# Cross attention's matmuls in three fp32r products of halves, another order of the first loads, and the last FFN's sums in one product each

## What is computed

```
for layer in 0, 1:
    x += 0.5 * ffn(rms_norm(x, g1))          # w_gu 1024 x 5632, w_down 2816 x 1024
    x += mixer(rms_norm(x, g2))              # attention, even or odd form
    x += cross(rms_norm(x, g3), rms_norm(mem, g4))
    x += 0.5 * ffn(rms_norm(x, g5))
x = second_block(x)                          # index attention, rnn, then an FFN

def cross(h, m):                             # m: 256 rows; 4 heads of 256
    q = rms_norm(h @ w_q, q_gain);  k, v = split(m @ w_kv);  k = rms_norm(k, k_gain)
    p = softmax(q @ k.T / 16)                # 512 x 256 per head
    return (p @ v) @ w_o
```

## Time and profile before

| | us |
|---|---|
| median of 3 runs | 3139.92 (3139.75 to 3141.52) |
| profiled execution, its own time | 3140.26 |
| its span in the trace | 3138.5 |
| TensorE busy in the span | 3117.4 |
| VectorE busy | 1580.1 |
| ScalarE busy | 1219.5 |
| cross stage of layer 0, on TensorE | about 678.8 to 712.3 |
| cross stage of layer 1, on TensorE | about 1819.7 to 1853.2 |

### The profile page before, as it was taken

One profiled execution on the slowest core, in us unless ns is written; L12 is line 12 of the kernel. 1 busy time (PEld: TensorE's weight loads), 2 busy tenths in 40 slices (PEclk: granted clock), 3 DMA queues, 4 the chain that ended last, 5 costly groups with the idle time before them and its releaser, 6 DMA issues.

```text
span 3138.5 us, 37126 instructions
## 1 busy us (share of the span) xinstructions
PE 3117.4 (99%) x14528; PEld 2520.7 (80%) x14528; DVE 1580.1 (50%) x2478; ACT 1219.5 (39%) x2001; POOL 314.4 (10%) x452
## 2 busy tenths in 40 slices
PE   9999999999999999999999999999999999999999
PEld 8888886887888888888866878888887786788887
DVE  4443348754444344433465754443346876564433
ACT  4332347543332233223465543332335727433222
POOL 1000114211000000001210200000142200020000
PEclk9999999999999999999999999999999999999999
DMA  4332331422333233323222413332232230223332
GB/s 152 99 96 95 100 94 35 141 68 88 101 95 100 94 94 94 101 99 96 88 94 81 148 49 99 100 96 96 84 101 81 81 108 28 88 80 95 96 99 74
DMA packets 213664, 290.95 MB, mean 93 GB/s; under 512 B 12880, under 2 KB 137168, under 8 KB 213360
## 3 DMA queue, kind: packets, MB, share of 16 engines
q1 hardware_dynamic: 210992, 279.59, 28.4%
q0 software_dynamic: 2496, 8.98, 0.9%
HBM read 286.42 MB, written 2.10 MB: 92 GB/s over the span
## 4 chain that ended last, share of the span: by engine, by line
PE 93%; issue 3%; ACT 1%; POOL 1%; DVE 1%; DMA 0%; SPq 0%; POOLq 0%; DVEq 0%
PE ps L94 91%; PE ps L97 3%; POOL evQ L142 0%; ACT sxPb L100 0%; ACT ocPb L100 0%; POOL evPb L142 0%; DMA x_rows<-in_x 0%; ACT sxPa L100 0%; ACT ocPa L100 0%; POOL evPa L142 0%; DVE ocPa L106 0%; DVE sxPa L106 0%; DVE evQ L115 0%; ACT ocPT L100 0%; ACT sxPT L100 0%
## 5 line engine op out<-in xcount | busy, mean ns | idle before, releaser
L103 DVE TENSOR_TENSOR wl<-raw,wh 128x1024 fp32r<-128x1024 f32 (+1 forms) x530 | 653.8, 1241 | 1070.9 <-ACT wh L100 1068.3
L100 ACT ACTIVATE wh<-raw 128x1024 fp32r<-128x1024 f32 (+1 forms) x530 | 551.7, 1050 | 1146.2 <-PE ps L94 1108.6
L94 PE MATMUL ps<-hTh,wh 128*128 128x512 f32 x2400 | 943.2, 393 | 1.8 <-DVE hTl L109 1.8
L94 PE MATMUL ps<-hTh,wl 128*128 128x512 f32 x2400 | 937.4, 391 | 0.0
L94 PE MATMUL ps<-hTl,wh 128*128 128x512 f32 x2400 | 937.3, 391 | 0.0
L94 PEld LDWEIGHTS ps<-hTh,wh 128*128 128x128 f32 x2400 | 450.9, 188 | 104.7 <-issue 11.0
L94 PEld LDWEIGHTS ps<-hTh,wl 128*128 128x128 f32 x2400 | 450.8, 188 | 96.9 <-issue 5.0
L94 PEld LDWEIGHTS ps<-hTl,wh 128*128 128x128 f32 x2400 | 450.9, 188 | 96.0 <-issue 5.9
L103 POOL TENSOR_TENSOR xn<-xn 128x512 f32<-128x512 f32 x67 | 95.9, 1431 | 1768.4 <-ACT xn L100 1529.6
L94 PE MATMUL ps<-wh,hTh 128*128 128x512 f32 (+2 forms) x576 | 217.4, 377 | 0.9 <-DVE s_ikT L121 0.9
L94 PE MATMUL ps<-wh,hTl 128*128 128x512 f32 (+2 forms) x576 | 216.0, 375 | 0.0
(11 more groups left out here) (418 smaller groups left out, 4068.1 us busy)
## 6 DMA issues: line engine op xcount, KB each, us to landing
raw<-in_ffn_w_gu SPq DMA_DIRECT2D x352, 256.0 KB, 3.1
raw<-in_ffn_w_down SPq DMA_DIRECT2D x88, 512.0 KB, 3.5
raw<-in_xa_w_kv SPq DMA_DIRECT2D x32, 512.0 KB, 3.9
raw<-in_w_in SPq DMA_DIRECT2D x28, 512.0 KB, 3.7
raw<-in_od_w_in SPq DMA_DIRECT2D x24, 512.0 KB, 3.6
raw<-in_w_ffn_gate SPq DMA_DIRECT2D x44, 256.0 KB, 2.8
raw<-in_w_ffn_up SPq DMA_DIRECT2D x44, 256.0 KB, 3.1
raw<-in_w_ffn_down SPq DMA_DIRECT2D x22, 512.0 KB, 3.8
```

The source lines that it names most:

```text
L94: return self.made(lambda e: e.matmul(*a, **k))
L100: return self.made(lambda e: e.activation(*a, **k))
L103: return self.made(lambda e: e.tensor_tensor(*a, **k))
```

## The change

- *Cross attention.* `qT`, `kT`, `v` and `PT` become pairs of fp32r tiles, upper and lower. ScalarE writes all upper halves, VectorE all lower halves, each after ScalarE's (`act_halves`, `dve_halves`, `act_whole_turned`, `dve_whole_turned`). Each fp32 matmul of scores and values becomes three fp32r products. `P` and `PT` move to memory that is free by then.
- *Order of products.* In group 0 of every GEMM the two products with the activations' upper half come first for all columns, and wait for the upper half only; the one with the lower half comes after.
- *Start.* SP loads x's first quarter, half a chunk of weights and x's second quarter, then waits for x's first quarter; ScalarE's own queue loads the other half of chunk 0, the identity and the first gains. Chunk 0 is split in halves. Two chunks of x are turned before the first product, two after product 12, four after product 36; 14 matmuls on ones.
- *Last FFN.* GpSimd adds all eight squares, and TensorE makes 4 matmuls in place of 12, after product 82.

```diff
     def sp_weights(sp):
+        sp.dma_start(x_rows[:, :, 0:256], x_in_rows[:, :, 0:256]).then_inc(x_in[0], 0, 16)
+        first_weights(sp, 1)
+        sp.dma_start(x_rows[:, :, 256:512], x_in_rows[:, :, 256:512]).then_inc(x_in[1], 0, 16)
+        sp.wait_ge(x_in[0], 0)
...
+    def act_loads(act):
+        first_weights(act, 0)
+        act.dma_start(ident, T["misc"][:, 0:P]).then_inc(ident_in, 0, 16)
+        act.dma_start(prm[:, 0:8], T["prm"][:, 0:8]).then_inc(prm_in, "first gain", 16)
...
+                if not g and len(block) == 1:
+                    order = [(k, j, qs) for k in ks for qs in ([range(3)] if k[0] == K - 1 else [range(2), range(2, 3)])
+                             for j in range(len(jobs))]
...
-        pe_warm(pe, home["f1u0", 0], 18)
-        pe_turn_x(pe, range(4))
-        pe_gemm(pe, "f1u0", {"h": hT("f1u0")}, side)
+        pe_warm(pe, home["f1u0", 0], 14)
+        pe_turn_x(pe, range(2))
+        side = rates_side(pe_rates, pe, "f1u0")
+        for i, _ in enumerate(pe_products(pe, "f1u0", {"h": hT("f1u0")}, side), 1):
+            if i == 12:
+                pe_turn_x(pe, range(2, 4))
+            elif i == 36:
+                pe_turn_x(pe, range(4, KD))
...
+    def act_whole_turned(act, A, h):
+        for n in range(2):
+            act.wait_ge(turned, (A.tag, h, n))
+            if h >= 2:
+                act.wait_ge(valued, (A.tag, h - 2))
+            for d_, s_ in whole_blocks(A, h, n, 0):
+                ins = act.activation(d_, s_, AF.Copy)
+            ins.then_inc(put, (A.tag, h, n, "hi"))
+
+    def dve_whole_turned(dve, A, h):
+        for n in range(2):
+            dve.wait_ge(put, (A.tag, h, n, "hi"))
+            if h >= 2:
+                dve.wait_ge(valued, (A.tag, h - 2))
+            for (d_, s_), (hi, _) in zip(whole_blocks(A, h, n, 1), whole_blocks(A, h, n, 0)):
+                ins = dve.tensor_tensor(d_, s_, hi.bitcast(F32), ALU.subtract)
+            ins.then_inc(put, (A.tag, h, n)).also(drained, (A.tag, h, "t", n))
...
+    def act_halves(act, name, g, nt, dst, gain):
+        for c in range(4):
+            act.wait_ge(turned, (name, g, c))
+            act.activation(dst[0][:, 4 * (g % 2) + c, :], bank[home[name, g] + c][:, 0:nt * P], AF.Copy,
+                           scale=gain[:, c % 2:c % 2 + 1]).then_inc(put, (name, g, "hi", c))
+
+    def dve_halves(dve, name, g, nt, dst, gain):
+        for c in range(4):
+            dve.wait_ge(put, (name, g, "hi", c))
+            dve.scalar_tensor_tensor(dst[1][:, 4 * (g % 2) + c, :], bank[home[name, g] + c][:, 0:nt * P],
+                                     gain[:, c % 2:c % 2 + 1], dst[0][:, 4 * (g % 2) + c, :].bitcast(F32), ALU.mult,
+                                     ALU.subtract).then_inc(put, (name, g, "T", c)).also(drained, ("turn", name, g, c))
...
-                ins = pe.matmul(dst, C.qT[:, u, i * P:(i + 1) * P], C.kT[:, u, :], start=c == 0, stop=c == 1)
+                for n, (a, b) in enumerate(((0, 0), (0, 1), (1, 0))):
+                    ins = pe.matmul(dst, C.qT[a][:, u, i * P:(i + 1) * P], C.kT[b][:, u, :], start=c == 0 and n == 0,
+                                    stop=c == 1 and n == 2)
...
-        pe_gemm(pe, "f3u", {"h": hT("f3u")}, rates_side(pe_rates, pe, "f3u"))
+        side = rates_side(pe_rates, pe, "f3u")
+        for i, _ in enumerate(pe_products(pe, "f3u", {"h": hT("f3u")}, side), 1):
+            if i == 82:
+                pe_sums(pe, "f3u", rate_bank("f3u"), [(total, step, ("f3u", "sum", KD - 1))], (1,))
...
-        pool_sums(pool, "f3u", KD - 2)
+        pool_sums(pool, "f3u")
```

More of the change, by code:

```diff
@@ L400, in sp_weights, with act_first, dve_first @@
                 o += width
+    def act_first(act, kk):
+        key = 0 if kk else "half"
+        act.wait_ge(raw_in[0], key)
+        act.activation(wh[0][:, kk, 0:chunk(0)], raw[0][:, kk, 0:chunk(0)], AF.Copy).then_inc(w_hi, key)
+        act.split = 1
+    def dve_first(dve, kk):
+        key = 0 if kk else "half"
+        dve.wait_ge(raw_in[0], key)
+        dve.wait_ge(w_hi, key)
+        dve.tensor_tensor(wl[0][:, kk, 0:chunk(0)], raw[0][:, kk, 0:chunk(0)], wh[0][:, kk, 0:chunk(0)].bitcast(F32),
+                          ALU.subtract).then_inc(w_lo, key)
+        dve.split = 1
     def act_split(act, upto):
@@ L622, in pe_rates @@
     def pe_rates(pe, N, g, kp):
[L623 to L627, removed]
+        if (g, kp) == (0, 2) and N not in ("f1u0", "f3u"):
+            pe_sums(pe, N, rate_bank(N), [(total, step, (N, "sum", KD - 1))], (1,))
         if (g, kp) == (0, 3) and N not in no_spread:
@@ L680, in upper @@
             act.wait_ge(turned, ("x", c))
-            act.wait_ge(prm_in, 0)
+            act.wait_ge(prm_in, "first gain")
             act_hi(act, bank[x_bank(c)][:, :], hT("f1u0"), c, slice(0, S), None, norm_gain["f1u0"][:, c:c + 1])
         def square(t):
-            act.wait_ge(x_in[0], 0)
-            act.wait_ge(x_in[1], 0)
+            for part in x_in:
+                act.wait_ge(part, 0)
             if t:
@@ L713, in keep @@
             dve.tensor_copy(xT[:, c, :], bank[x_bank(c)][:, :]).then_inc(x_ready, ("x", c)).also(drained, ("x", c))
-        dve_split(dve, 0)
-        for c in (0, 1, 2, 3):
+        dve_first(dve, 0)
+        lower(0)
+        dve_first(dve, 1)
+        lower(1)
+        for c in (0, 1):
+            keep(c)
+        dve_split(dve, 1)
+        for c in (2, 3):
             lower(c)
-        keep(0)
-        dve_split(dve, 1)
-        for c in (1, 2, 3):
+        for c in (2, 3):
             keep(c)
@@ L1276, in pe_whole, with whole_blocks @@
                 value(pe, s - 2, A.pt[s % 2])
[L1278 to L1282, removed]
+    def whole_blocks(A, h, n, u):
+        src, at = bank[A.tv + n], 0
+        for i in A.groups[n]:
+            k0, k1, _, W = WHOLE[i]
+            yield A.pt[h % 2][u][:, k0:k1, i * P:(i + 1) * P], src[:, at:at + W].rearrange("p (k q) -> p k q", k=k1 - k0)
+            at += W
+    def act_whole_turned(act, A, h):
[14 more added lines that the diff above has]
+            ins.then_inc(put, (A.tag, h, n)).also(drained, (A.tag, h, "t", n))
     def act_whole(act, A, finish, then):
@@ L1946, in side @@
             if (g, kp) == (3, 1):
[L1947 removed]
+                act_halves(act, C.kv, 2, 2, C.kT, C.kgain)
         def evict(g):
@@ L1973, in evict @@
                 return
[L1974 to L1977 removed]
+            for t in range(2):
+                cols = slice(512 * g, 512 * (g + 1))
+                dve.wait_ge(put, (C.kv, "vh", g, t))
+                dve.tensor_tensor(C.vl[:, t, cols], bank[home[C.kv, g] + t][:, :], C.vh[:, t, cols].bitcast(F32),
+                                  ALU.subtract).then_inc(put, (C.kv, "v", g, t)).also(drained, (C.kv, g, t))
         dve_gemm(dve, C.kv, evict, side)
@@ L2054, in value @@
                 for kt in range(2):
-                    ins = pe.matmul(bank[b][:, :], C.v[:, kt, 256 * h + c * P:256 * h + (c + 1) * P], PTb[:, kt, :],
-                                    start=kt == 0, stop=kt == 1)
+                    cols = slice(256 * h + c * P, 256 * h + (c + 1) * P)
+                    for n, (v, p) in enumerate(((C.vh, 0), (C.vl, 0), (C.vh, 1))):
+                        ins = pe.matmul(bank[b][:, :], v[:, kt, cols], PTb[p][:, kt, :], start=kt == 0 and n == 0,
+                                        stop=kt == 1 and n == 2)
                 ins.then_inc(valued, (A.tag, h, c)).also(valued, (A.tag, h))
```

116 lines of the change are left out of this document (59 added, 57 removed).

## The result

The changed kernel takes 3148.64 us (median of 13 runs, 3146.95 to 3151.27), the kernel before beside it 3141.31 us (3138.70 to 3144.88). The ratio is 1.0023, with an interval of 1.0015 to 1.0030: slower by about 7 us, where 8.3 were forecast. The profiled execution has a span of 3145.2 us, 6.7 more than before.

The account below looks back on a forecast made before the run. TensorE was busy 3117.4 of 3138.5 us, but the ScalarE-VectorE loop was taken to decide the cross stage. Cross stages +14.2, start -3.5, last FFN -2.4 gave +8.3 on 3140.26: 3148.5, as median 3148.2 us; range 3143.5 to 3154.5.

Parts of the forecast that it names:

- Cross stage, the schedule: Cross attention stage: VectorE's steps wait for ScalarE's upper halves, so the stage ends 6.1 us later in each layer.
- exp(0) to exp(1): Cross stage: time from head 0's first exponential to head 1's, forecast near 8 us, with later distances near 6.9.
- the 256-wide subtraction: Cross stage, VectorE's lower halves: no measured price, taken as 0.36 us each, between 0.33 and 0.43.
- Cross stage, the clock: Cross stage, last values: TensorE's clock falls to half after holes, costing 1.0 us a layer, bounds 0 and 2.7.
- fall in every hole: Cross stages: the clock falls in every hole, or the start starves: 3151 to 3155 us; large end, chance 0.16.
- The start: Kernel start: turning of x begins at 7.1 instead of 10.57 us, a gain of 3.5 us, bounds 2.0 and 4.3.
- chunk 1's cover of 1 us: Start: weight chunk 1 arrives some 4 us later, split by 13.5 and needed at 14.8, so no loss.
- Last FFN: Last feed-forward part: earlier first product 1.2 us, fewer sums 1.8, 0.6 lost to GpSimd; gain 2.4, bounds 1.5 and 3.3.
- Upstream: Copies of v and kT: one more 512-wide step per group on ScalarE and VectorE, priced 0, up to 0.5 us.
- TensorE as the bound: Rival for the cross stages: TensorE stays the bound, the stages save 9.2 us, total 3124.8 us; chance 0.08.
- a hand-over under 1.6 us a round: Cross stage: condition for TensorE staying the bound, that handing over from ScalarE to VectorE costs the loop under 1.6 us.
- ScalarE's table load: Start, rival: the 1.28 us load stands ahead of ScalarE's DMAs, the start gains nothing, 3151.7 us; within the large end's 0.16.

Follow-up runs that it names:

- filled holes: The changed kernel with unread matmuls on ones (12, 5 and 9) ahead of the turns of P of heads 0, 1 and 3: 3148.28 us, ratio 1.0019.
- the cross stage alone: The kernel before with only the change's cross attention; start, order of products and last FFN's sums as before: 3155.67 us, ratio 1.0045.
- late q: The changed kernel with VectorE's lower halves of q's second half moved behind head 1's and head 2's maxima, two each: 3143.74 us, one run.
- start and order alone: The kernel before with only the change's start and order of products; cross attention and last FFN's 12 sums as before: 3138.67 us, ratio 0.9989.
- two and two order with the early table: The changed kernel with q's halves written in pairs, P's upper halves ahead of the exponentials, and one early exponential loading the table: 3132.30 us, ratio 0.9969.

## Why the prediction was right, point by point

- **Cross stage, the schedule.** Forecast +6.1 a layer, found +6.34 and +6.30. exp(0) started unchanged against the first score; exp(0) to exp(1) was laid out at 8 us and took 8.10, then 6.85 and 7.4 against 6.75 and 7.36. So exp(0) to exp(3) is 22.21 us, laid out at 22.3. The term whose price no row of before showed, the 256-wide subtraction, is four in 1.42 us; with one of them some 0.41 long that is a spacing of (1.42 - 0.41) / 3, some 0.335, the low bound and not the 0.36 that I took. That would give +5.8. The remaining 0.5 lies behind exp(3), laid out at 11.4 us and taking 11.89: the last two heads' values take 714.92 - 708.88 = 6.04 us where I had 4 x 1.36 = 5.44. The second set starts 0.60 us behind the last product of the first, not 0.23, because it waits for the output's lower halves, one more hand-over from ScalarE to VectorE. (In the working, 2 x (7.2 + 2.7) is 19.8 and not 19; no choice hangs on it.)
- **Cross stage, the clock.** Forecast 1.0 a layer; this is the mis-sized term. In the profiled execution of the changed kernel it cost nothing: the granted clock fell only in the middle, where the chain holds no matmul and where the distances are those of the kernel with filled holes (clock 1.00), and from 704 to 714 us it is 1.00. The granted clock fell once per stage, behind the longest hole:

```profile
684.00:686.00 2.00, 0.00 (x0) 0.00 (x0) 2.00 (x4) 1.06 (x2) 0.00 (x0) 1.00 0.00 0
686.00:688.00 2.00, 1.29 (x6) 1.32 (x7) 1.97 (x9) 0.00 (x0) 0.00 (x0) 0.67 0.00 0
688.00:690.00 2.00, 2.00 (x12) 2.00 (x11) 0.85 (x4) 1.08 (x5) 0.00 (x0) 0.50 0.00 0
```

  That is the turn of P(0) and head 2's scores, with slack behind them: the wait for P(1) is 1.25 us here, and 2.75 in the cross stage alone, where the clock did not fall before it. I had put the fall into the last values. In two other kernels it came there in layer 0, and cost 1.5 us (the cross stage alone, +7.86 against +6.29 in its own layer 1; late q, +5.39 against +3.93), within the 0 to 2.7 that I gave. Whether it did so in the changed kernel's other runs, whose median is 1.7 us above the profiled one, no trace shows. The rival's fall in every hole did not come: here it came behind one of three holes over 1.2 us, and in the cross stage alone not behind holes of 2.89 and 2.75 us. The half clock that costs is the one on the path, not each one.
- **The start.** Forecast -3.5, found -3.39. But two of its steps were off and cancelled in this execution. The turning started at 6.49 instead of 7.1, and the first product at 8.64 (I had said 8.5). The wait in this execution is not for x:

```profile
6.49 1.09 PE L97 MATMUL ps<-misc,x_rows 128*128 128x128 f32 x8 [0.64 <-DMA misc<-in_misc]
7.81 0.69 ACT L100 ACTIVATE hTh<-ps,prm 128x512 fp32r<-128x512 f32 x1 [1.43 <-DMA prm<-in_prm]
8.64 0.47 PE L94 MATMUL ps<-hTh,wh 128*128 128x512 f32 x1 [1.06 <-ACT hTh L100]
```

  It is for the identity (64 KB) and then for the first gains, the smallest and last load of ScalarE's queue. The turning is 4.08 us earlier than before, the first product 4.21, and 0.8 of that is lost on the way to 412.30. The start moves from run to run: in the other eleven kernels that have it the turning starts between 5.81 and 7.33 us, right behind the warming matmuls and with no wait shown, and the step at 412.30 stands between 411.07 and 412.62; the old start gave 417.12 in the cross stage alone, not 415.69. So a gain of 3.1 to 6 us is what these traces allow, and the agreement within 0.1 is luck. ScalarE's queue added no bandwidth that shows: from 4 to 6 us 345 GB/s were moved, against 352; only from 2 to 4 us it was 279 against 189. That chunk 1's cover of 1 us would hold was right: its split on VectorE starts at 11.65 and TensorE does not wait for it.
- **Last FFN.** Forecast -2.4, found -2.34. The sums stand where laid out, with a wait for GpSimd of 0.83 where I had 0.6:

```profile
2793.34 1.05 PE L94 MATMUL ps<-ones,xn 128*128 128x1 f32 x8 [0.83 <-POOL xn L103]
```

  What I missed is that the two gains can depend on each other (start and order alone).
- **Upstream** price 0: the distances between the common steps outside the stretches agree within 0.18 us, apart from the attention stage's 0.45.
- **Sum.** With the found terms it is 12.64 - 3.39 - 2.34 = +6.9 instead of +8.3. The median landed at the forecast because the kernel before, in the larger set of runs, took 3141.3 and not the 3139.9 that I started from: 1.4 us of the hit are luck. The change itself was forecast at +8.3 and measured at +7.3.
- **Rivals.** TensorE as the bound would have been 9 us faster in the stages; it failed at its own condition, a hand-over under 1.6 us a round, which cost 3.2 and 1.9 in the first two rounds. In the third it cost 0.4, since that round took 6.95 before and not the 4.88 that I took for the loop. The two and two order with the early table shows that this rival was reachable only in part: 2.5 of the 9 us. Even there the stage is 32.4 us and TensorE works 29.1 of them, not the 27.6 laid out. ScalarE's table load did not stand ahead of its DMAs.

## What to carry over

Splitting an operand into an upper and a lower half makes two engines that worked side by side into a chain, and each copy that was halved between them becomes a round trip. Lay out the loop of the feeding engines with the new order before counting what TensorE saves, and then move the first half of the round trip ahead of the long operation of its engine. When a step is moved, list what else it signals: here it drained a bank, and the first instruction of a kind carried a table load with it.

## What the runs showed of the hardware

- In the kernel before, the output projection's first fp32r product, right behind fp32 values, has a record of 0.79 us and the next starts 0.63 us after it, where the distance is else 0.23. In the changed kernel the values are fp32r and the step is gone (0.39, next after 0.22), which saves 0.4 us per layer. The stretches count this; the stage's length from first score to first product does not (+6.77 there, +6.34 in the stretch). Behind turnings the step is smaller, 0.31 us to the next product.
- Half clock for 25 us in a stage of 38.8, with a third of the products, changed the distances of the loop by 0.01 us; half clock for 3.4 us in the last values cost 1.5.
- Holes of equal length did not have equal effect on the clock: 2.89 us without a fall and 2.29 us with one in the same stage (the cross stage alone, layer 0), and 2.89 us with one in its layer 1. What decides it stays open; no run was made for that.
- A load of 4 KB issued fourth on ScalarE's queue landed some 5.4 us after its issue began, beside the 1.6 MB of the start. ScalarE's issues take 0.45 to 0.5 us each there, and its table load (1.28 us) came behind them, at 2.81.
